# Latent attention with queries in twelve tiles: rotary rows of four heads in one tile, turned with DMA copies and tables, then copied to their heads

## The chip, the cores and the metric

The kernel runs on one core of one Trainium2 chip. The metric is the time of one launch in microseconds of device time. The core has TensorE (PE: matmuls, and their weight loads, PEld), VectorE (DVE), ScalarE (ACT), GpSimd (POOL) and SyncE (SP, which issues most of the DMAs). Each engine works through its own list of instructions in order and waits on semaphores where the list says so.

## The reference

The program has two blocks. The change lies in the first, in the second layer of it, where the mixer is latent attention with 16 heads. For a sequence of 512 positions with 1024 features:

```python
def mla_queries(h, w_q_a, q_a_norm, w_q_b, q_nope_norm, q_rope_norm, cos, sin):
    c_q = rms_norm(h @ w_q_a, q_a_norm)
    q = (c_q @ w_q_b).reshape(bsz, seq, N_HEADS, QK_DIM)
    q_nope = rms_norm(q[..., :QK_NOPE_DIM], q_nope_norm)
    q_rope = apply_rope(rms_norm(q[..., QK_NOPE_DIM:], q_rope_norm), cos[:, :, None, :], sin[:, :, None, :])
    return jnp.concatenate([q_nope, q_rope], axis=-1).transpose(0, 2, 1, 3)

def apply_rope(x, cos, sin):
    x1, x2 = jnp.split(x.astype(jnp.float32), 2, axis=-1)
    return jnp.concatenate([x1 * cos - x2 * sin, x1 * sin + x2 * cos], axis=-1).astype(x.dtype)
```

A head's query has 64 rows without position ("nope") and 32 rotary ones ("rope"). Keys are made likewise, with one rotary part shared by all heads. Then comes causal softmax attention over blocks of 128 queries, and the output product with `w_o`. All of it is in float32.

## The kernel before

Activations lie with features on the 128 partitions and the 512 positions along the row, so one tile is 128x512. A float32 product is made of three matmuls on split values: each weight block is split into a high part `wh` (ScalarE, line 678) and a low part `wl` (VectorE, line 1253), and `product` (lines 2027 to 2029) runs high by high, high by low and low by high for each of its row blocks: three blocks for queries (nine matmuls), two for keys (six). Loads of weight blocks are in a ring of four, the split parts in a ring of two, so block b + 2 can be split only when block b has been used. `ahead(st, i, u, last)` is the split of block u + 2. The blocks of this stage ("b") stand in `BLOCKS_B`.

A query tile of one head has its 64 nope rows, its 32 rope rows, and 32 rows more in which the rope rows stand exchanged (the weights hold them twice). So there is one tile for each head, 16 in all, and the rotation needs no movement: the tile is multiplied by a table (`qtab`), and the doubled rows are summed by the score matmul itself, since the keys hold the shared rope rows twice. One key tile holds the nope rows of two heads (8 tiles).

The order is written out by hand for each engine. For head h, TensorE does: the product for head h + 2 (`head_queries`), then for each of four blocks j of queries `turn_probs(h, j)` (transposes, line 2268) and `scores(h + 1, j)` (lines 2254, 2255); behind j = 1 the mean square of the new query tile by a matmul (`query_mean`, line 2325), in even heads the weighing of values (line 2282), in odd heads the key product of a later pair and its mean (line 2331). ScalarE makes squares (lines 940, 945), inverse roots (lines 702, 703), exponentials (line 874) and copies of transposed probabilities (line 966). VectorE makes the row minima (`row_least`, line 1574; scores are kept negated), the shares (`share_first`, `share_probs`, line 1584: probabilities divided by their sum), queries (`head_queries`, lines 1669, 1671) and keys (`head_keys`, line 1676). `turn_probs(h, 0)` on TensorE needs the first share of head h, and the shares of head h stand behind `row_least(h, 3)` in VectorE's list; this is the loop through which each head hangs on the one before. In VectorE's list for head h stand, in order:

```python
                    share_first(h)
                    ahead(st, 0, AT_B["q", h + 2], True)
                    row_least(h + 1, 0)
                    row_least(h + 1, 1)
                take_sums(h, slice(3, 4))
                share_probs(h, 3)
                    output_low(pair - 1)
                    head_queries(h + 2)
                    row_least(h + 1, 2)
                copy_turned(h)
                    row_least(h + 1, 3)
```

(some conditions left out). Bank 2 of the matmul memory takes query tiles, bank 3 key tiles, bank 7 all means. In the last two heads TensorE also begins the output product (`output_part(u, ks)`, lines 2366 to 2368; a step is one of eight row blocks of one of eight tiles, three matmuls). GpSimd does nothing in this stage.

## Time and profile before

| | |
|---|---|
| median of 3 runs (lowest, highest) | 1868.06 us (1867.62, 1868.92) |
| the profiled execution: its time | 1866.67 us |
| the profiled execution: its span | 1864.6 us |
| mean granted TensorE clock | 0.99 |
| TensorE busy | 1810.5 us (97%) |
| VectorE, ScalarE, GpSimd busy | 1041.5, 839.4, 199.6 us |

The span reaches from the first to the last instruction that the profiler saw; the time has what lies around it too. The rows of the trace below are of the profiled execution. A row of the timeline gives the start from the beginning of the span and the duration, both in microseconds, then the engine, the line, the operation, output and inputs, the shape and how many instructions are merged in it; in square brackets is the idle time before it and what ended it.

### The profile page before, as it was taken

How to read it: one execution, taken by the hardware profiler on the slowest of the kernel's cores; microseconds unless marked ns; L12 is line 12 of the kernel's file. 1: busy time of each engine (PE TensorE's matmuls, PEld its weight loads, DVE VectorE, ACT ScalarE, POOL GpSimd, SP SyncE). 2: the span in 40 equal slices, each digit the busy share in tenths (PEclk: the TensorE clock that was granted, in tenths of full speed). 3: DMA queues.
4: the chain of work that ended last, by engine and by line, in shares of the span. 5: the costliest groups of instructions: out<-in, count | busy, mean ns of one | idle time of the engine just before them, and what ended most of it. 6: DMA issues, size and time to landing. Idle time of an engine off the chain costs nothing.

```text
span 1864.6 us, 24367 instructions
## 1 busy us (share of the span) xinstructions
PE 1810.5 (97%) x8934; PEld 1395.1 (75%) x8934; DVE 1041.5 (56%) x1633; ACT 839.4 (45%) x1406; POOL 199.6 (11%) x269
## 2 busy tenths in 40 slices
PE   9889999999999999999999999999999989999997
PEld 6677778888887766677888888768666767866675
DVE  8874454444334767755444434465555476556647
ACT  5423344443224666644444422232567633265753
POOL 7970000000000000000000000023000012200000
PEclk9989999999999999999999999999999999999998
DMA  6322322323333111122232333323111122311111
GB/s 212 103 58 79 98 94 90 101 91 98 94 96 101 44 35 28 62 74 96 90 101 92 98 94 94 97 87 106 57 57 46 46 90 88 105 51 52 57 45 57
DMA packets 58764, 152.21 MB, mean 82 GB/s; under 512 B 17152, under 2 KB 22048, under 8 KB 58672
## 3 DMA queue, kind: packets, MB, share of 16 engines
q1 hardware_dynamic: 55120, 148.27, 25.3%
q0 software_dynamic: 3552, 2.70, 0.5%
q8 instruction: 59, 0.97, 0.2%
q14 instruction: 33, 0.27, 0.0%
HBM read 143.79 MB, written 4.19 MB: 79 GB/s over the span
## 4 chain that ended last, share of the span: by engine, by line
PE 88%; DVE 4%; ACT 3%; POOL 3%; issue 1%; DMA 0%; SPq 0%; DVEq 0%; ACTq 0%; POOLq 0%
PE bank L2027 19%; PE bank L2028 18%; PE bank L2029 18%; PE bank L2522 3%; PE bank L2524 3%; PE bank L2523 3%; PE bank L2499 2%; PE bank L2487 2%; PE bank L2486 2%; PE bank L2485 2%; PE bank L2254 1%; PE bank L2282 1%; PE bank L2609 1%; PE bank L2537 1%; PE bank L2506 1%
## 5 line engine op out<-in xcount | busy, mean ns | idle before, releaser
L1253 DVE TENSOR_TENSOR wl<-raw,wh 128x1024 fp32r<-128x1024 f32 (+3 forms) x280 | 324.1, 1158 | 493.9 <-ACT wh L678 490.7
L678 ACT ACTIVATE wh<-raw 128x1024 fp32r<-128x1024 f32 (+3 forms) x280 | 279.2, 997 | 573.5 <-PE bank L2029 498.0
L2027 PE MATMUL bank<-xH,wh 128*128 128x512 f32 x904 | 355.2, 393 | 3.9 <-DVE wl L1253 2.1
L2029 PE MATMUL bank<-xH,wl 128*128 128x512 f32 x904 | 352.1, 389 | 0.0
L2028 PE MATMUL bank<-xL,wh 128*128 128x512 f32 x904 | 352.1, 389 | 0.0
L2027 PEld LDWEIGHTS bank<-xH,wh 128*128 128x128 f32 x904 | 169.9, 188 | 43.4 <-DVE xL L1259 3.2
L2028 PEld LDWEIGHTS bank<-xL,wh 128*128 128x128 f32 x904 | 170.0, 188 | 35.6 <-issue 1.0
L2029 PEld LDWEIGHTS bank<-xH,wl 128*128 128x128 f32 x904 | 169.8, 188 | 35.5
L2027 PE MATMUL bank<-hidH,wh 128*128 128x512 f32 x352 | 137.3, 390 | 0.0
L2029 PE MATMUL bank<-hidH,wl 128*128 128x512 f32 x352 | 136.9, 389 | 0.0
L2028 PE MATMUL bank<-hidL,wh 128*128 128x512 f32 x352 | 136.9, 389 | 0.0
L2522 PE MATMUL bank<-xH,wh 128*128 128x512 f32 x256 | 108.4, 423 | 0.0
L2524 PE MATMUL bank<-xH,wl 128*128 128x512 f32 x256 | 100.8, 394 | 0.0
L2523 PE MATMUL bank<-xL,wh 128*128 128x512 f32 x256 | 100.2, 391 | 0.0
L614 POOL TENSOR_TENSOR xT<-xT,acc 128x512 f32<-128x512 f32 x9 | 11.2, 1273 | 737.1 <-ACT acc L1053 737.1
L1925 DVE TENSOR_REDUCE least<-bank 128x1 f32<-128x128 f32 (+3 forms) x96 | 42.6, 485 | 73.4 <-PE bank L2506 73.3
L1109 ACT ACTIVATE Pm<-bank,least 128x128 f32<-128x128 f32 (+3 forms) x96 | 49.8, 524 | 68.3 <-DVE least L1925 68.3
L2028 PEld LDWEIGHTS bank<-hidL,wh 128*128 128x128 f32 x352 | 66.1, 188 | 14.0 <-issue 0.2
L2027 PEld LDWEIGHTS bank<-hidH,wh 128*128 128x128 f32 x352 | 66.1, 188 | 13.9 <-issue 0.2
L2029 PEld LDWEIGHTS bank<-hidH,wl 128*128 128x128 f32 x352 | 66.1, 188 | 13.7
L861 ACT ACTIVATE hidH<-T 128x512 f32 (+1 forms) x44 | 27.8, 632 | 78.3 <-DVEq L1541 78.3
L604 POOL COPY xT<-T 128x512 f32<-128x512 f32 x8 | 8.8, 1105 | 453.3 <-DVE T L1559 453.3
(450 smaller groups left out, 3305.6 us busy)
## 6 DMA issues: line engine op xcount, KB each, us to landing
raw<-w_gu_dram SPq DMA_DIRECT2D x88, 512.0 KB, 3.3
raw<-w_p_dram SPq DMA_DIRECT2D x64, 512.0 KB, 3.4
raw<-w_dn_dram SPq DMA_DIRECT2D x32, 448.0 KB, 3.3
raw<-w_glu_dram SPq DMA_DIRECT2D x16, 512.0 KB, 3.5
raw<-w_dn_dram SPq DMA_DIRECT2D x16, 512.0 KB, 3.5
raw<-w_out_dram SPq DMA_DIRECT2D x16, 512.0 KB, 3.3
raw<-w_in_dram SPq DMA_DIRECT2D x8, 512.0 KB, 7.8
raw<-w_o_dram SPq DMA_DIRECT2D x8, 512.0 KB, 3.4
```

Of the source, the lines that this page charges most:

```text
L678: nc.scalar.activation(wh[:, (st.base + u) % 2, 0:kts * P], raw[:, (st.base + u) % 4, 0:kts * P], ACT.Copy).then_inc(w_high, 1)
L1109: nc.scalar.activation(Pm[side][:, POFF[j]:POFF[j] + w], banks[side][:, 0:w], ACT.Exp, scale=-1.0, bias=least[:, j, side:side + 1], accum_ ...
L1253: nc.vector.tensor_tensor(wl[:, s, 0:kts * P], raw[:, (st.base + u) % 4, 0:kts * P], wh[:, s, 0:kts * P].bitcast(F32), ALU.subtract).then_ ...
L1925: nc.vector.tensor_reduce(least[:, j, side:side + 1], banks[side][:, 0:(j + 1) * P], AX, ALU.min)\
L2027: nc.tensor.matmul(bank, wh[:, s, w], hi[:, k, :], start=first and kt == 0, stop=False)
L2028: nc.tensor.matmul(bank, wh[:, s, w], lo[:, k, :], start=False, stop=False)
L2029: ins = nc.tensor.matmul(bank, wl[:, s, w], hi[:, k, :], start=False, stop=last and kt == kts - 1)
L2485: nc.tensor.matmul(o, xH[:, k, rows], wh[:, s, w], start=k == 0, stop=False)
L2486: nc.tensor.matmul(o, xH[:, k, rows], wl[:, s, w], start=False, stop=False)
L2522: nc.tensor.matmul(bank, wh[:, s, w], xH[:, kt, :], start=kt == 0, stop=False)
L2523: nc.tensor.matmul(bank, wh[:, s, w], xL[:, kt, :], start=False, stop=False)
L2524: ins = nc.tensor.matmul(bank, wl[:, s, w], xH[:, kt, :], start=False, stop=kt == KD - 1)
```

## The change

Queries are packed without doubled rows. Eight tiles ("n") hold the nope rows of two heads each, four tiles ("r") the rope rows of four heads each: first halves of the four heads in the upper 64 rows, second halves in the lower 64. That makes 12 query tiles. The nope halves go from the bank straight to the heads' query tiles (`take_queries`, two operations over 64 rows). A rope tile is taken with its norm to `rope_q` (`take_rope`), GpSimd issues two DMA copies that write its halves exchanged to `rope_x`, VectorE multiplies both by tables and adds them (`turn_rope`), and GpSimd issues eight DMA copies of 16 rows that place the result in four heads' query tiles, four for each pair. The tables are built from the sine table by sixteen DMA copies. The query tiles are now four instead of two, with the unused rows zeroed once. TensorE's order gives a head one projection from `MAIN` (rope tile 1 for head 0, then nope queries in odd heads and keys in even ones), and heads 3 and 7 a second one from `SECOND` (rope tiles 2 and 3); output steps begin in head 13. The means take one matmul for each tile as before. Scores wait for `rope_placed` too.

```diff
-BLOCKS_B = [("q", 0), ("k", 0), ("v", 0), ("v", 1), ("q", 1), ("k", 1)]
-for _p in range(1, NH // 2):
-    BLOCKS_B += [("q", 2 * _p), ("q", 2 * _p + 1)] + [("k", _p + 1)] * (_p + 1 < NH // 2)
+BLOCKS_B = [("r", 0), ("k", 0), ("v", 0), ("n", 0), ("v", 1), ("k", 1), ("n", 1), ("r", 1), ("n", 2), ("k", 2), ("n", 3),
+            ("r", 2), ("k", 3), ("n", 4), ("k", 4), ("n", 5), ("r", 3), ("k", 5), ("n", 6), ("k", 6), ("n", 7), ("k", 7)]
+IN_BANK2 = [("r", 0)] + [("n", p) for p in range(NH // 2)]
+IN_BANK3 = [b for b in BLOCKS_B if b[0] != "v" and b not in IN_BANK2]
+NORMED = [b for b in BLOCKS_B if b[0] != "v"]
+MAIN = dict(enumerate([("r", 1)] + [(kind, p) for p in range(2, NH // 2) for kind in "nk"]))
+SECOND = {3: ("r", 2), 7: ("r", 3)}
 AT_B = {kind: n for n, kind in enumerate(BLOCKS_B)}
...
-    qst = [mla.tensor(f"qst{b}", [P, S]) for b in range(2)]
+    qst = [[mla.tensor(f"qst{s}", [P, S])[:, :] for s in range(2)], [sq[:, s, :] for s in range(2)]]
     qtab = [mla.tensor(f"qtab{s}", [P, S]) for s in range(2)]
+    rope_q, rope_x = T[:, 1, :], sd[:, :]
...
             pool.dma_start(posI[:, :], pos.to_broadcast([P, S])).then_inc(sem("pos_loaded"), 16)
             pool.dma_start(means[:, :], con[:, CON["mean_even"][0]:CON["fold"][1]]).then_inc(sem("means_loaded"), 16)
+            pool.wait_ge(sem("rope_table"), 1)
+            for n in range(8):
+                to = slice(n * DR // 2, (n + 1) * DR // 2)
+                turning = DN + DR + n // 4 * DR // 2
+                pool.dma_start(qtab[0][to, :], ropeT[DN:DN + DR // 2, :]).then_inc(sem("rope_rows1"), 16)
+                pool.dma_start(qtab[1][to, :], ropeT[turning:turning + DR // 2, :]).then_inc(sem("rope_rows1"), 16)
+            for g in range(NH // 4):
+                pool.wait_ge(sem("roped"), 2 * g + 1)
+                for half in range(2):
+                    pool.dma_start(rope_x[half * DN:(half + 1) * DN, :], rope_q[(1 - half) * DN:(2 - half) * DN, :])\
+                        .then_inc(sem("rope_rows0"), 16)
+                pool.wait_ge(sem("roped"), 2 * g + 2)
+                for pair in range(2 * g, 2 * g + 2):
+                    if pair >= 2:
+                        pool.wait_ge(sem("scores_ready"), 8 * pair - 8)
+                    for s in range(2):
+                        for half in range(2):
+                            to = (DN, 0)[s] + half * DR // 2
+                            at = half * DN + (2 * (pair % 2) + s) * DR // 2
+                            pool.dma_start(qst[pair % 2][s][to:to + DR // 2, :], rope_q[at:at + DR // 2, :])\
+                                .then_inc(sem(f"rope_placed{pair % 2}"), 16)
...
+            for n, name in enumerate(("q_nope", "q_rope")):
+                step(nc.vector.tensor_scalar(tiny[:, 24 + n:25 + n], column(name), -scale, None, ALU.mult))
+            for tile in qst:
+                step(nc.vector.memset(tile[0][DN + DR:P, :], 0.0))
+                step(nc.vector.memset(tile[1][DR:DN, :], 0.0))
+
+            def take_rope(g):
+                bank, i = taken_from(("r", g))
+                if g:
+                    for n in range(2):
+                        dve.wait_ge(sem(f"rope_placed{n}"), 64 * g)
+                dve.wait_ge(sem("rq_ready" if bank == 2 else "rk_ready"), i + 1)
+                nc.vector.scalar_tensor_tensor(rope_q, banks[bank][:, :], tiny[:, 25:26], (R if bank == 2 else acc)[:, :], ALU.mult, ALU.mult)\
+                    .then_inc(sem("roped"), 1)
+                dve.wait_ge(sem("roped"), 2 * g + 1)
+                dve.sem_inc(sem("q_used" if bank == 2 else "kv_used"), 1)
+
+            def turn_rope(g):
+                if g == 0:
+                    dve.wait_ge(sem("rope_rows1"), 256)
+                dve.wait_ge(sem("rope_rows0"), 32 * (g + 1))
+                step(nc.vector.tensor_tensor(rope_q, rope_q, qtab[0][:, :], ALU.mult))
+                step(nc.vector.tensor_tensor(rope_x, rope_x, qtab[1][:, :], ALU.mult))
+                nc.vector.tensor_tensor(rope_q, rope_q, rope_x, ALU.add).then_inc(sem("roped"), 1)
+
+            take_rope(0)
+            dve.wait_ge(sem("krope_folded"), 1)
             dve.wait_ge(sem("krope_folded"), 1)
             def rope_rows(p):
                 step(nc.vector.tensor_copy(kst[p][0][bottom, :], banks[6][bottom, :]))
                 step(nc.vector.tensor_copy(kst[p][1][top, :], banks[6][top, :]))
             rope_rows(0)
-            def head_queries(h):
-                s = h % 2
-                dve.wait_ge(sem("rq_ready"), h + 1)
-                step(nc.vector.tensor_tensor(qst[s][:, :], banks[2][:, :], R[:, :], ALU.mult))
+            def take_queries(pair):
+                dve.wait_ge(sem("rq_ready"), taken_from(("n", pair))[1] + 1)
+                for s, rows in enumerate((top, bottom)):
+                    step(nc.vector.scalar_tensor_tensor(qst[pair % 2][s][rows, :], banks[2][rows, :], tiny[rows, 24:25], R[rows, :],
+                                                        ALU.mult, ALU.mult))
                 dve.sem_inc(sem("q_used"), 1)
-                nc.vector.tensor_tensor(qst[s][:, :], qst[s][:, :], qtab[s][:, :], ALU.mult).then_inc(sem("qk_ready"), 1)
-
...
-                if h + 2 < NH:
-                    head_queries(h + 2)
-                if s and pair + 2 < NH // 2:
-                    ahead(st, 0, AT_B["k", pair + 2], True)
+                if h in MAIN:
+                    take(MAIN[h])
+                if h in SECOND:
+                    ahead(st, 0, AT_B[SECOND[h]], True)
+                if h in (1, 4, 8):
+                    turn_rope(1 + h // 4)
                 if h + 1 < NH:
                     row_least(h + 1, 2)
                 copy_turned(h)
                 if h + 1 < NH:
                     row_least(h + 1, 3)
+                if h in SECOND:
+                    take(SECOND[h])
...
+                sooner = NORMED[0:NORMED.index(item)]
+                pe.wait_ge(sem("qsq_ready" if bank == 2 else "ksq_ready"), i + 1)
+                if sooner:
+                    pe.wait_ge(sem("rq_ready"), sum(b in IN_BANK2 for b in sooner))
+                    if any(b in IN_BANK3 for b in sooner):
+                        pe.wait_ge(sem("rk_ready"), sum(b in IN_BANK3 for b in sooner))
                 else:
                     pe.wait_ge(sem("latroot_ready"), 3)
-                nc.tensor.matmul(banks[7][:, :], mean_of("mean_odd" if h % 2 else "mean_even"), T[:, 0, :], start=True, stop=True)\
-                  .then_inc(sem("qstat_ready"), 1)
-
-            def key_mean(pair):
-                pe.wait_ge(sem("ksq_ready"), pair + 1)
-                pe.wait_ge(sem("rq_ready"), max(2 * pair, 1))
-                nc.tensor.matmul(banks[7][:, :], mean_of("mean_pair"), T[:, 2, :], start=True, stop=True)\
-                  .then_inc(sem("kstat_ready"), 1)
+                mean = mean_of("mean_rope" if item[0] == "r" else "mean_pair")
+                nc.tensor.matmul(banks[7][:, :], mean, T[:, 0 if bank == 2 else 2, :], start=True, stop=True)\
+                  .then_inc(sem("qstat_ready" if bank == 2 else "kstat_ready"), 1)
             def values(m):
...
                 for j in range(QT):
                     turn_probs(h, j)
                     if h + 1 < NH:
                         scores(h + 1, j)
-                    if j == 1 and h + 2 < NH:
-                        query_mean(h + 2)
+                    if j == 1 and h in MAIN:
+                        mean_square(MAIN[h])
                     if pair and s == 0 and j in (1, 2):
                         weigh(pair - 1, range(2 * j - 2, 2 * j))
-                    if s and pair + 2 < NH // 2:
+                    if h in SECOND:
                         if j == 1:
-                            pair_keys(pair + 2)
+                            projected(SECOND[h])
                         if j == 2:
-                            key_mean(pair + 2)
+                            mean_square(SECOND[h])
                     if h == NH - 2 and j == 3:
                         output_part(0, range(4, 6))
                     if h == NH - 1 and j % 2:
-                        output_part(1, range(j - 1, j + 1))
+                        output_part(1, range(j + 1, j + 3) if j == 1 else range(4, 5))
             weigh(NH // 2 - 1, range(QT))
-            output_part(0, range(6, KD))
-            output_part(1, range(4, KD))
+            output_part(0, range(6, 7))
+            output_part(1, range(5, 7))
```

TensorE in odd head 5, from the mean behind j = 1: before, the six matmuls of a key product (`cvH`, `cvL`) and at the end its mean stand among turns and scores.

```order
L2325 MATMUL bank<-T,means 128x512 [waits rk_ready,rq_ready,qsq_ready]
L2027 MATMUL bank<-cvH,wh 128x512 [waits w_split,kv_used]
L2028 MATMUL bank<-cvL,wh 128x512
L2029 MATMUL bank<-cvH,wl 128x512
L2027 MATMUL bank<-cvH,wh 128x512
L2028 MATMUL bank<-cvL,wh 128x512
L2029 MATMUL bank<-cvH,wl 128x512
L2268 MATMUL bank<-cons,Pb_103 128x128 [waits turned_act,probs_shared]
L2268 MATMUL bank<-cons,Pb_103 128x128 x2
L2254 MATMUL bank<-kst_120,qst_122 128x384 [waits probs_ready]
L2255 MATMUL bank<-causal,minus_unit 128x128
L2331 MATMUL bank<-T,means 128x512 [waits rq_ready,ksq_ready]
```

After, nothing stands there, and the key product comes once the head is done:

```order
L2393 MATMUL bank<-T,means 128x512 [waits rk_ready,rq_ready,qsq_ready]
L2334 MATMUL bank<-cons,Pb_103 128x128 [waits turned_act,probs_shared]
L2334 MATMUL bank<-cons,Pb_103 128x128 x2
L2320 MATMUL bank<-kst_120,sq 128x384 [waits probs_ready]
L2321 MATMUL bank<-causal,minus_unit 128x128
L2334 MATMUL bank<-cons,Pb_103 128x128 [waits turned_act,probs_shared]
L2334 MATMUL bank<-cons,Pb_103 128x128 x3
L2320 MATMUL bank<-kst_120,sq 128x512 [waits probs_ready]
L2321 MATMUL bank<-causal,minus_unit 128x128
L2092 MATMUL bank<-cvH,wh 128x512 [waits w_split,kv_used]
```

The product and the mean have moved to the even heads, and the query product that opened the even head now opens the odd one.

VectorE in head 3, from the queries to the first shares of head 4 (`Pb`), before:

```order
L1669 TENSOR_TENSOR qst_123<-bank,R 128x512 [waits rq_ready]
L1671 TENSOR_TENSOR qst_123<-qst_123,qtab_125 128x512 [waits dve_steps]
L1253 TENSOR_TENSOR wl<-raw,wh 128x384 [waits w_high]
L1574 TENSOR_REDUCE nmax<-bank 128x1 [waits scores_ready]
L1592 COPY PTc<-bank 128x4x128 [waits transposed]
L1574 TENSOR_REDUCE nmax<-bank 128x1 [waits scores_ready]
L1579 RECIPROCAL rden<-den 128x3 [waits probs_ready]
L1584 TENSOR_SCALAR Pb_102<-Pb_102,rden 128x128 [waits dve_steps]
```

and after, where lines 1602, 1607, 1612 and 1620 are the minimum, the reciprocal, the share and the copy:

```order
L1720 SCALAR_TENSOR_TENSOR sq<-bank,tiny,R 64x512 [waits rq_ready]
L1720 SCALAR_TENSOR_TENSOR sq<-bank,tiny,R 64x512 [waits dve_steps]
L1282 TENSOR_TENSOR wl<-raw,wh 128x384 [waits dve_steps,w_high]
L1602 TENSOR_REDUCE nmax<-bank 128x1 [waits scores_ready]
L1620 COPY PTc<-bank 128x4x128 [waits transposed]
L1602 TENSOR_REDUCE nmax<-bank 128x1 [waits scores_ready]
L1696 SCALAR_TENSOR_TENSOR T<-bank,tiny,acc 128x512 [waits rk_ready,rope_placed1,rope_placed0]
L1607 RECIPROCAL rden<-den 128x3 [waits roped,probs_ready]
L1612 TENSOR_SCALAR Pb_102<-Pb_102,rden 128x128 [waits dve_steps]
```

The third line from the end is new: `take_rope(2)`, which waits for its own root (`rk_ready`), stands between the last minimum and the shares.

GpSimd behind the loads of this stage, before (the next is work of the second block):

```order
L607 DMA posI_117<-pos_dram 128x512 [waits hid_used0]
L608 DMA means_127<-con_dram 128x512
L614 TENSOR_TENSOR xT_49<-xT_49,acc_59 128x512 [waits ln_sq,ln_delta_copied]
L614 TENSOR_TENSOR xT_49<-xT_49,acc_59 128x512 x2
L619 DMA rope_cos_144<-con_dram 128x512
```

and after, from the last two of the sixteen table copies on:

```order
L621 DMA qtab0_124<-ropeT_116 16x512
L622 DMA qtab1_125<-ropeT_116 16x512
L626 DMA sd_60<-T_62 64x512 [waits roped]
L626 DMA sd_60<-T_62 64x512
L636 DMA qst0_122<-T_62 16x512 [waits roped]
L636 DMA qst0_122<-T_62 16x512
L636 DMA qst1_123<-T_62 16x512 x2
L636 DMA sq_61<-T_62 16x512 x4
```

The exchange waits for `roped` once, the placing copies once more; pair 0's four and pair 1's four follow one another.

## Rows read from the trace of the kernel before

**Rows 1.** The page, part 1: busy time, share of the span, instructions.

```profile
PE 1810.5 (97%) x8934; PEld 1395.1 (75%) x8934; DVE 1041.5 (56%) x1633; ACT 839.4 (45%) x1406; POOL 199.6 (11%) x269
```

**Rows 2.** Windows: one pair of heads, busy time (instructions), clock, DMA share, GB/s.

```profile
713.87:732.69 18.82, 18.46 (x92) 12.02 (x91) 13.89 (x34) 13.30 (x35) 0.00 (x0) 1.00 0.11 29
```

**Rows 3.** Timeline, TensorE: start, us, line, form, count; heads 3 and 4.

```profile
686.92 0.45 PE L2027 MATMUL bank<-cqH,wh 128*128 128x512 f32 x1
...
689.08 0.27 PE L2268 MATMUL bank<-cons,Pb 128*128 128x128 f32 x1
...
690.21 1.07 PE L2325 MATMUL bank<-T,means 128*128 128x512 f32 x2
...
694.09 1.13 PE L2331 MATMUL bank<-T,means 128*128 128x512 f32 x2 [0.36 <-ACT T L945]
...
698.55 0.27 PE L2268 MATMUL bank<-cons,Pb 128*128 128x128 f32 x1
```

**Rows 4.** Timeline, VectorE: one large split, then heads 2 and 3.

```profile
635.48 1.23 DVE L1253 TENSOR_TENSOR wl<-raw,wh 128x1024 fp32r<-128x1024 f32 x1
...
682.33 1.53 DVE L1676 SCALAR_TENSOR_TENSOR kst<-bank,vecs,acc 64x512 f32<-64x512 f32 x2
684.01 0.69 DVE L1669 TENSOR_TENSOR qst<-bank,R 128x512 f32<-128x512 f32 x1
684.85 0.69 DVE L1671 TENSOR_TENSOR qst<-qst,qtab 128x512 f32<-128x512 f32 x1
...
690.80 0.61 DVE L1574 TENSOR_REDUCE nmax<-bank 128x1 f32<-128x128 f32 x2
...
693.58 0.69 DVE L1669 TENSOR_TENSOR qst<-bank,R 128x512 f32<-128x512 f32 x1 [0.98 <-ACT R L703]
...
695.50 0.55 DVE L1574 TENSOR_REDUCE nmax<-bank 128x1 f32<-128x384 f32 x1
...
697.41 0.88 DVE L1584 TENSOR_SCALAR Pb<-Pb,rden 128x128 f32<-128x128 f32 x3
```

**Rows 5.** Timeline, TensorE: a mean, first scores, turn of head 1.

```profile
631.45 1.02 PE L2294 MATMUL bank<-sq,means 128*128 128x512 f32 x2
632.33 0.47 PE L2027 MATMUL bank<-cvH,wh 128*128 128x512 f32 x1
...
646.10 0.38 PE L2254 MATMUL bank<-kst,qst 128*128 128x128 f32 x2
...
670.22 0.33 PE L2268 MATMUL bank<-cons,Pb 128*128 128x128 f32 x1 [0.48 <-DVE Pb L1584]
```

**Rows 6.** Timeline, ScalarE: the sine of the rotary table, a large split.

```profile
619.21 0.63 ACT L917 ACTIVATE ropeT<-ropeT 128x512 f32<-128x512 f32 x1
...
634.39 1.05 ACT L678 ACTIVATE wh<-raw 128x1024 fp32r<-128x1024 f32 x1
```

**Rows 7.** Timeline, GpSimd: one of sixteen issues in a row.

```profile
1289.00 0.50 POOL L639 DMA_DIRECT2D cq_exact<-fg_low  x1
```

**Rows 8.** DMA issues: copies between rows, KB each, median us to landing.

```profile
acc<-qk POOLq DMA_DIRECT2D x32, 16.0 KB, 3.2
```

**Rows 9.** Timeline, TensorE: turn of head 13, last output steps, the product behind.

```profile
783.18 0.27 PE L2268 MATMUL bank<-cons,Pb 128*128 128x128 f32 x1
...
807.55 0.50 PE L2366 MATMUL bank<-kvH,wh 128*128 128x512 f32 x1 [0.53 <-DVE kvL L1702]
...
811.26 0.38 PE L2428 MATMUL bank<-tiny,cons 64*128 64x4 f32 x2
```

**Rows 10.** Timeline, TensorE: two gaps earlier in the kernel.

```profile
69.70 1.89 PE L2079 MATMUL bank<-G,C 128*32 128x128 f32 x32 [2.74 <-DVEq L1419]
...
149.55 0.47 PE L2027 MATMUL bank<-zH,wh 128*128 128x512 f32 x1 [1.16 <-DVE wl L1253]
```

**Rows 11.** Windows behind these gaps; the number after POOL is the clock.

```profile
69.00:74.00 5.00, 4.30 (x39) 3.27 (x40) 4.62 (x6) 0.39 (x1) 4.84 (x3) 0.66 0.15 56
148.00:153.00 5.00, 3.84 (x17) 2.85 (x16) 3.81 (x4) 3.09 (x4) 0.00 (x0) 1.00 0.44 129
```

254 lines of the change are left out of this document (132 added, 122 removed).

## The prediction

> **What bounds the kernel now.** I read the page first: TensorE is busy 1810.5 of 1864.6 us, VectorE 56%, ScalarE 45% [rows 1]. So what counts is the TensorE work that goes and the waits that come, in the attention stage, 632 to 811 us. Next the windows by pair of heads: in steady state a pair takes 18.82 us, TensorE 18.46 of them, VectorE 13.89, ScalarE 13.30 [rows 2]. TensorE binds, but the other two are at 74% and 71%, and they work in series on one chain per head, so I followed that chain in the timelines.
>
> TensorE in odd head 3 [rows 3]: a query product starts at 686.92, the turning of the head's probabilities (line 2268, "turn") at 689.08, the mean square at 690.21, then come the pair's key product (six matmuls for nine: 1.44 us) and, after a wait of 0.36, its mean at 694.09, the next query product, and the next turn at 698.55. Turn to turn is 9.47 us; the even half of a pair is 18.82 less that, 9.35.
>
> The chain in the same head, in VectorE's timeline [rows 4]: ScalarE squares the finished product and splits the next weights; then VectorE reads row minima at 690.80 (1.7 behind the turn); ScalarE takes two exponentials and the root; VectorE forms the queries at 693.58 (2.78 behind the minima). Behind them in its queue stand a weight split, the minimum of the third score row (695.50), a copy, the last minimum and the shares (697.41); a third of these 0.88 us lets the next turn go, at about 697.72. So the chain is 8.65 us from turn to turn, 0.8 shorter than TensorE's work. That 0.8 is all the cover there is.
>
> **What is removed.** Four query tiles. A tile costs TensorE 686.92 to 689.08, 2.16 us, and its mean 631.45 to 632.33, 0.88 [rows 3, 5]. 4 x 3.04 = 12.2 us. If TensorE stayed full, the profiled execution's 1866.67 would become 1854.5. VectorE counts level: 16 x 2 operations of 128x512 make room for 8 x 2 half-height and 4 x 4 full ones, and four splits go. Half height buys nothing: the pair's two key operations over 64 rows take 682.33 to 684.01, 1.68 us, as two full ones do [rows 4].
>
> **What moves, and why the gain does not come through.** The new order gives a head one projection: nope queries in odd heads, keys in even ones, and rotary tiles beside them in heads 3 and 7. An even head keeps its weighing of values and is followed by a query product: 9.35 us of TensorE as before, above the chain. An odd head has lost its key product, its key mean and (the next product being keys) a third of a query product: 9.47 - 1.44 - 0.9 - 0.36 - 0.7 = 6.1 us of work (the terms: key product, mean, its wait, 2.16 - 1.44). Its chain is hardly shorter: the 8.65 of before, less the split and the two operations in front of the minimum (695.50 - 693.58 = 1.92), plus 1.68 for the halves: 8.4. So the odd head takes 8.4, with TensorE idle about 2.4 just before each turn.
> - Plain pairs (heads 5 and 6, 9 and 10): 8.4 + 9.35 = 17.8, 1.0 less than before: -2.0. Heads 11 and 12: the odd one has no split and takes 7.6, the even one waits 0.5 for its squares behind the large split, and 4 steps of the output product are moved here (+0.7): 18.2, -0.7.
> - Pairs with a rotary tile (3 and 4, 7 and 8): in the odd head the rotary product (2.16) delays the third score row, a split (0.47) goes in front of its minimum, and before the shares VectorE must wait for a second root and then take the tile (0.8): the root cannot start before the third exponential, 7.8 us behind the turn, ends at 9.1, the take at 10.0, the turn at 10.5. In the even head, taking keys (1.68) is followed by the turning, three 128x512 operations at 0.84, 0.84 and 0.61 (684.01 to 684.85 is the first of such [rows 4]): 2.3 more before the minima, so that the chain there, about 9.9, passes TensorE's 9.35. 20.4 for the pair: +1.6 each, +3.2.
> - Heads 1 and 2: the turning is in the odd head: 8.4 + 2.3 - 0.1 = 10.6, and 9.35: +1.1.
>
> Heads 1 to 12 together: +1.6.
>
> **The start.** Work moves forward: up to head 1's turn TensorE does seven tiles, not six, and one mean more: +3.0. On top come new waits. Block 4 (the second half of the values) can be split only when block 2 is used up, at 643, not at 634: ready at 645.4 by 1.05 us on ScalarE and 1.23 on VectorE [rows 4, 6]. The first rotary tile is taken by 639.4 (its root ends at 638.0 as the first root does now, four memsets stand before it), its two swap copies are issued in 1.0 and land by 643.5, the turning stands behind that split in VectorE's queue, ends 647.7, and four copies to the heads take 2.0 to issue. One GpSimd copy issue holds 0.50 us, and a copy from rows to rows lands 3.2 us after its issue [rows 7, 8]: 652.5. TensorE has by then just finished the values, so first scores come at 652.5 for 646.10 [rows 5], with almost no wait for the copies. Then the mean of tile (n, 1) must wait until the root of (k, 1) has freed the bank, behind the third exponential of head 0: 2.8 us idle near 660. Head 1's turn I get at 674.5, against 670.22 [rows 5]: +4.3.
>
> The sixteen table copies start when the sine is done (619.85 [rows 6]) and need 8.0 + 3.2: 631, long before 645. The later rotary tiles are copied a head or more before their scores; their wait is hidden by about 9 us of other work, and would cost the exposed 4 x 0.5 + 3.2 = 5.2 each if that went. The Trainium skill (DMA: Bandwidth & Descriptors, Anatomy of one DMA) puts a GpSimd copy at about 2.0 us plus bytes over 436 GB/s, so 2.1 for 32 KB; the trace's 3.2 disagrees upward and is what I use; by the page nothing in the sum would move, because the values end at 652.4 anyway.
>
> **The tail.** From head 13's turn (783.18) to the last output step (811.26, the small product behind it) are 28.1 us [rows 9]. Of these go the last query mean (0.88), the four output steps now done before that turn (2.85), the 0.53 at 807.55 for the low half of the last pair (three steps stand in front of it now, one before), and about 0.7 of small waits, among them that for the query bank: -5.0.
>
> **TensorE's clock.** In this kernel a gap of 2.74 us ended at 69.70, and 69 to 74 then ran at a mean granted clock of 0.66 (down to 1.2 GHz), a loss of 5 x 0.34 = 1.7 us; a gap of 1.16 at 149.55 left it at 1.00, 2.4 GHz [rows 10, 11]. In the attention stage the granted clock is 1.00 now [rows 2]. Head 1 gets one of 10.6 - 6.1 = 4.5, right before an even head that TensorE binds: +1.7. The one at 660 gives about +0.5 more. The odd gaps of 2.4 lie between the two observations, nearer to 2.74; I count them at nothing, and at 1.7 each in the range.
>
> **Sum.** +4.3 + 1.6 - 5.0 + 2.2 = +3.1 us on 1866.67. The median of the runs shown is 1868.06, 1.4 above the profiled execution, and the change goes on it: 1871. About 0.2% (3.7 us) is what a measurement of this kernel tells from no change.
>
> **Rivals.**
> - *TensorE stays full.* For it: 97% busy, every microsecond of work removed counts, and my odd-head chain has only to be 1.5 us shorter. Against: the cover of 0.8 us. All of it gives 1855.9; half of the removed work comes through if the two rotary pairs run like plain ones (-5.2) and the start costs only its work (-1.3, and no clock loss, -2.2): 1862. Chance 0.14.
> - *The clock falls in every odd head.* One mechanism: each odd gap of about 2.4 us lets the clock fall, and the even head behind it, bound by TensorE, starts slow. Heads 3, 5, 7, 9 and 11: up to 5 x 1.7 = 8.5, 1879; with two of them 1874. It decides from where half a drop more (0.8 us) is added. For it: 2.74 was enough. Against: 1.16 was not, and heads 3, 7 and 11 leave only 1.5 to 1.8. With errors of the start and the rotary pairs to the same side: 0.41.
> - *The copies come late.* If the four placing copies took 3 us more at the start, scores wait 3: 1874; later ones never show. It is inside the case above. The Trainium skill (same page, SWDGE vs HWDGE vs iDMA) says VectorE's two-port operations keep GpSimd from writing descriptors; that would stretch the 0.50 us of an issue. The row shows 0.50; no run here shows it beside such operations.
> - *Forecast:* the waits eat the gain, 1867 to 1871.8: 0.45.
>
> Range: 1863 to 1877. It leaves the full gain and four or more clock drops outside.
>
> **What would show it.** Right: pairs of about 17.8 (plain) and 20.4 (rotary) us; TensorE idle released by VectorE's shares at the turns of heads 2, 4, 6, 8, 10; first scores 21 us behind the first product's end; a low clock after head 1's gap; the tail 5 us shorter. Wrong: a pair under 17 us (chain overestimated), a wait on the rope copies at a score row (copies late), or clock below 1.00 after each odd head.

## The result and the profile after

The changed kernel takes 1885.13 us (median of 4 runs, 1881.43 to 1886.83), the kernel before 1867.84 beside it (4 runs): ratio 1.0086, 95% interval 1.0074 to 1.0098. It is slower by 17.3 us; the forecast was 3 slower, 1871, in a range that ended at 1877. One execution among all those reported below, in the third kernel of experiments 9 to 11, took 2565.27 us at a mean granted clock of 0.65 and stays out of every comparison.

The profiled execution of after takes 1886.83 us, its span 1885.0 (before 1866.67 and 1864.6). Page, part 1, as in [rows 1]:

```profile
PE 1812.5 (96%) x8890; PEld 1394.4 (74%) x8890; DVE 1044.3 (55%) x1631; ACT 832.0 (44%) x1389; POOL 228.0 (12%) x325
```

There are 44 matmuls fewer, and TensorE is busy 2 us longer: less work, more time for it. The next rows say where; "..." stands for rows left out, here and in all that follows. They are TensorE's timeline of after: the stage's first mean, the first scores, gaps, and the first turn (one transpose, L2334) of heads 1, 2, 3, 4, 6, 7, 10 and 13; then the small product behind the output and the product after it.

```profile
635.40 0.59 PE L2360 MATMUL bank<-sq,means 128*128 128x512 f32 x1
...
656.90 0.46 PE L2320 MATMUL bank<-kst,qst 128*128 128x128 f32 x2 [0.41 <-PE bank L2409]
...
665.75 0.67 PE L2393 MATMUL bank<-T,means 128*128 128x512 f32 x1 [2.69 <-ACT acc L732]
...
678.89 0.33 PE L2334 MATMUL bank<-cons,Pb 128*128 128x128 f32 x1 [0.67 <-DVE Pb L1612]
...
689.60 0.48 PE L2334 MATMUL bank<-cons,Pb 128*128 128x128 f32 x1 [4.34 <-DVE Pb L1612]
...
701.17 0.27 PE L2334 MATMUL bank<-cons,Pb 128*128 128x128 f32 x1
...
711.30 0.80 PE L2092 MATMUL bank<-cvH,wh 128*128 128x512 f32 x1 [2.54 <-DVEq L1699]
...
714.03 0.41 PE L2334 MATMUL bank<-cons,Pb 128*128 128x128 f32 x1
...
733.55 0.33 PE L2334 MATMUL bank<-cons,Pb 128*128 128x128 f32 x1 [2.29 <-DVE Pb L1612]
...
744.71 0.27 PE L2334 MATMUL bank<-cons,Pb 128*128 128x128 f32 x1
...
776.79 0.33 PE L2334 MATMUL bank<-cons,Pb 128*128 128x128 f32 x1 [2.30 <-DVE Pb L1612]
...
804.76 0.27 PE L2334 MATMUL bank<-cons,Pb 128*128 128x128 f32 x1
...
828.06 0.27 PE L2495 MATMUL bank<-tiny,cons 64*128 64x4 f32 x1
...
829.99 0.47 PE L2092 MATMUL bank<-kvH,wh 128*128 128x512 f32 x1 [1.55 <-DVE wl L1282]
```

Against the same marks of before (631.45, 670.22, 783.18 and 811.26, [rows 5, 9]):

| part | before | after | difference | forecast |
|---|---|---|---|---|
| up to the stage's first mean | 631.45 | 635.40 | +3.95 | 0 |
| from there to head 1's turn | 38.77 | 43.49 | +4.7 | +4.3 |
| head 1's turn to head 13's | 112.96 | 125.87 | +12.9 | +3.3 with the clock |
| head 13's turn to the small product | 28.08 | 23.30 | -4.8 | -5.0 |
| from there to the end (1866.67, 1886.83) | 1055.41 | 1058.77 | +3.4 | 0 |

The forecast's other 0.5 was clock at the start; it belongs to the second row, where the clock did fall (0.64 from 665.75 to 669.75). Start and tail came out as worked out. The middle is four times what was forecast, and two parts that had no term cost 7.3. Call the stretch from first mean to small product the stage: 179.8 us before, 192.7 after.

The clock in after: windows of 4 us (TensorE busy, granted clock, DMA share, GB/s), and one over the stage.

```profile
686.00:690.00 4.00, 0.40 (x2) 0.67 0.11 25
690.00:694.00 4.00, 4.00 (x13) 0.50 0.21 57
694.00:698.00 4.00, 4.00 (x26) 0.98 0.00 0
710.00:714.00 4.00, 2.69 (x6) 0.65 0.29 67
734.00:738.00 4.00, 4.00 (x14) 0.64 0.19 53
777.00:781.00 4.00, 4.00 (x21) 1.00 0.39 111
832.00:836.00 4.00, 4.00 (x14) 0.74 0.33 109
632.00:824.00 192.00, 169.44 (x764) 0.95 0.17 46
```

Behind the gap of 4.34 TensorE was full for 4 us at 0.50, that is 1.2 GHz for 2.4, and did half the work. The clock fell too, for a part of their windows, behind the gaps of 2.54 and 2.29, and behind the 1.55 that ended at 829.99, but not behind the 2.30 that ended at 776.79. Before had 1.00 all through the stage.

### The profile page after: what moved, and what is told of

Its sections match the earlier page's. It is cut to its first block, busy times and chain, and to the rows that moved or that the text cites. A ratio compares the mean times of both kernels' runs of the same rounds, so it can differ in the third digit from the quotient of the medians.

```text
span 1885.0 us, 24327 instructions
## 1 busy us (share of the span) xinstructions
PE 1812.5 (96%) x8890; PEld 1394.4 (74%) x8890; DVE 1044.3 (55%) x1631; ACT 832.0 (44%) x1389; POOL 228.0 (12%) x325
## 4 chain that ended last, share of the span: by engine, by line
PE 84%; DVE 7%; ACT 4%; POOL 3%; issue 2%; DMA 0%; SPq 0%; DVEq 0%; ACTq 0%; POOLq 0%
PE bank L2092 18%; PE bank L2093 18%; PE bank L2094 18%; PE bank L2589 3%; PE bank L2591 3%; PE bank L2590 3%; PE bank L2566 2%; PE bank L2552 2%; PE bank L2554 2%; PE bank L2553 2%; DVE wl L1282 1%; PE bank L2676 1%; PE bank L2604 1%; PE bank L2320 1%; PE bank L2573 1%
```

## Experiments

Eleven kernels and a second trace of the kernel before. Stage times are read as above, in each run's own trace. A head is measured from its own first turn to the next head's.

### 1. Two waits taken away by order

VectorE and ScalarE handle the second tile of heads 3 and 7 sooner, and the output product ends its first block sooner:

```diff
+                    if j == 2 and h in SECOND:
+                        root_of(SECOND[h])
                     if h + 1 < NH:
                         probs(h + 1, 1 - s, j)
...
-                    if j == 2 and h in SECOND:
-                        root_of(SECOND[h])
...
                     row_least(h + 1, 2)
+                if h in SECOND:
+                    take(SECOND[h])
                 copy_turned(h)
                 if h + 1 < NH:
                     row_least(h + 1, 3)
-                if h in SECOND:
-                    take(SECOND[h])
...
-            output_part(1, range(5, 7))
+            output_part(1, range(5, 6))
             output_part(0, range(7, KD))
-            output_part(1, range(7, KD))
+            output_part(1, range(6, KD))
```

> Two waits of the changed kernel that the prediction did not have are taken away by order alone. (1) In heads 3 and 7 ScalarE forms the rotary tile's root before the third exponential (it sat idle 1.50 us there) and VectorE takes the tile before the copy and the fourth minimum, so bank 3 comes free about 2 us sooner for the key product of heads 4 and 8, whose gap is 2.54 us now. (2) At the end block 0 of the output product is finished three steps before block 1, so the split of block 2 is ready sooner (gap 1.55 us now). Theory 'the two waits and the clock fall behind each are most of the excess': the gaps at heads 4 and 8 fall to 0.5 us, the granted clock stays at 1.00 in 710 to 718 and 754 to 762, each pair with a rotary tile is 2 to 3 us shorter, the tail 1 to 2; in all 5 to 8 us less behind the start of the stage. Rival 'the chain of VectorE sets the head anyway, the product only fills its idle time': the gap moves from in front of the key product to in front of the next turn, 0 to 2 us less. On the part before the stage both say nothing; if its extra 4 us against the kernel before are chance they need not come back here.

Measured: 1879.74 us in one run, stage 190.2 (2.5 less), heads 1 to 13 123.3 (2.6 less), from the small product to the end 1055.45, the 1055.41 of before. The key product's gap, and the one behind the output (no clock fall follows it now):

```profile
708.83 0.50 PE L2092 MATMUL bank<-cvH,wh 128*128 128x512 f32 x1 [1.03 <-DVEq L1699]
...
825.53 0.47 PE L2092 MATMUL bank<-kvH,wh 128*128 128x512 f32 x1 [0.85 <-DVE wl L1282]
```

Heads 3 and 4 take 20.8 us for 23.2, heads 7 and 8 20.9 for 22.9; against that stands a fall of the clock in head 10 (11.19 for 9.55), which moved here. Behind the output the next product starts 1.24 us after the small one, for 1.93 in after and 0.31 in before: 1.6 of the 3.4 there were the wait, and 0.9 of it is left; another 1.5 was the fall of the clock. The small rest, 0.3, arises later, where the executions differ by themselves (see 9 to 11), and that is also why this trace ends level with before. Both waits are real. The total fell by 5.8 us, within the 5 to 8 of the first theory, though the two gaps fell to 1.03 and not to 0.5; the rival allowed at most 2.

### 2. The gaps filled with products that nobody needs

```diff
+            def filler(count, pair):
+                if count and pair > 1:
+                    pe.wait_ge(h_ready, 32 + pair - 1)
+                for _ in range(count):
+                    nc.tensor.matmul(banks[6][:, :], const("ones"), cons[:, 0:S], start=True, stop=True)
```

> The changed kernel with extra products into a bank that is free (ones times constants, 0.59 us each, nothing reads them) in the seven gaps of TensorE from the start of the stage to head 12: 4 ahead of the second nope tile's mean, 7 ahead of head 2's turn, 4 ahead of the key products of heads 4 and 8, 3, 3 and 2 ahead of the turns of heads 6, 10 and 12. Nothing else changes, so the chains stay as long as they are. Theory 'the clock': with no gap the granted clock stays at 1.00 all through the stage, and what the gaps cost behind them comes back: 1.7 us or more for each of the six falls of this part (666 to 762 us), stage 6 to 9 us shorter. Rival 'the waits alone': the clock may stay up but the chains on VectorE and ScalarE set the end, stage shorter by less than 2 us or even longer by the fillers that end late.

Measured: 1880.60 us in one run, stage 189.8, 2.9 less. One window over the stage, of this kernel:

```profile
640.00:820.00 180.00, 174.14 (x790) 1.00 0.15 43
```

The clock theory's first half holds: TensorE is busy 174 of 180 us here (169 of 192 in after's window above), and was done sooner with more to do. The heads behind a gap show it: head 2 takes 9.35 us for 11.57, head 6 9.39 for 11.16. The size was missed (2.9 for 6 to 9), because a filler is two instructions and took 0.86 us, not 0.59 (seven took 6.01). So the seven ahead of head 2's turn made head 1 take 12.2 for 10.7, and the four ahead of head 4's key product made head 3 12.3 (head 7 too; with the wait but no fall it takes 11.64, as in experiment 4). Experiment 5 repeats it with numbers that fit.

### 3. No rotation

The three VectorE operations of `turn_rope` (line 1699 on) are left out, so queries go unrotated to their heads.

> Leaves out the rotation of the queries: the three VectorE operations over 128x512 per group of four heads (12 in all); the copies stay. Theory 'the rotation stands in the chain of its head': heads 1, 4 and 8 are each about 2.2 us shorter (0.72+0.72+0.72), and the first score rows come up to 2.2 us sooner. Rival 'hidden': the even heads 4 and 8 are bound by TensorE or by the wait for bank 3, so they get under 1 us shorter; only head 1 gains. Everything from head 9 on as it was.

Measured: 1877.46 us in one run, stage 189.4; head 1 8.76 us for 10.71, head 4 9.63 for 10.37, head 8 9.87 for 10.68. The first scores came 21.5 us behind the first mean, as in after: they wait for the last of the values in both (0.41, the row at 656.90 of after). So the rival was right of the even heads, and the rotation costs nothing at the start.

Neither theory had the next thing: heads 5 and 9, which have no rotation, take 8.62 and 8.61 us for 9.15. ScalarE's last exponential of head 9 and its part of the weight split, and VectorE's first minimum (head 9's turn stands at 758.36):

```profile
757.12 0.69 ACT L903 ACTIVATE Pb<-bank,nmax 128x512 f32<-128x512 f32 x1 [1.29 <-DVE nmax L1602]
...
759.05 0.52 ACT L707 ACTIVATE wh<-raw 128x384 fp32r<-128x384 f32 x1
```

```profile
760.07 0.61 DVE L1602 TENSOR_REDUCE nmax<-bank 128x1 f32<-128x128 f32 x2
```

and the same two of ScalarE in after (turn at 767.64):

```profile
767.22 0.69 ACT L903 ACTIVATE Pb<-bank,nmax 128x512 f32<-128x512 f32 x1 [0.52 <-DVE nmax L1602]
...
768.85 0.53 ACT L707 ACTIVATE wh<-raw 128x384 fp32r<-128x384 f32 x1
```

Without the rotation TensorE's own work sets the end of head 8, as it did in before: the exponential starts 1.24 us ahead of the turn, the split 0.69 behind it, the minimum 1.71 behind it, the 1.7 of [rows 3, 4]. With it the shares set that end (0.20 idle at the turn of head 9, 0.57 at that of head 5), the exponential starts only 0.42 ahead, the split 1.21 behind, the minimum 2.25 behind. So the rotation costs 4.6 us in five heads (1.95, 0.74, 0.53, 0.81, 0.54); the stage is only 3.3 shorter, since the clock fell in heads 10 and 12 instead of head 6.

### 4. Twice the copies

```diff
+                            pool.dma_start(ropeT[at:at + DR // 2, :], rope_q[at:at + DR // 2, :])\
+                                .then_inc(sem(f"rope_placed{pair % 2}"), 16)
                             pool.dma_start(qst[pair % 2][s][to:to + DR // 2, :], rope_q[at:at + DR // 2, :])\
```

(the waits on `rope_placed` doubled).

> The changed kernel with each placing copy of GpSimd preceded by a second one of the same size and source into a tile that is free, so a pair of heads needs eight issues, not four. At the start the last copy lands about 2.0 us later (4 x 0.49). Theory 'no slack at the start, plenty later': first scores 1.5 to 2.5 us later, all heads from 1 on as long as they were, stage +2. Rival 'copies are on the path in the rotary heads too': heads 4, 5, 8 and 9 get longer by 1 us or more each. If they were hidden at the start as well: stage within 0.5 us.

Measured: 1886.27 us in one run, stage 192.0, 0.7 less than after, with one fall of the clock fewer. The first scores wait for the copies now, 21.9 us behind the first mean for 21.5:

```profile
656.99 0.35 PE L2324 MATMUL bank<-kst,qst 128*128 128x128 f32 x1 [0.79 <-DMA qst<-T]
```

Both theories missed in part: 2 us more of copies cost 0.4 at the start, not 1.5 to 2.5, and heads 4, 5, 8 and 9 did not get longer. The rows of after say why there was slack: a copy of 32 KB landed 1.8 us after its issue there (median of sixteen), not 3.2.

```profile
sd<-T POOLq DMA_DIRECT2D x8, 128.0 KB, 2.2
qst<-T POOLq DMA_DIRECT2D x16, 32.0 KB, 1.8
```

The rival of late copies is out. The Trainium skill (DMA: Bandwidth & Descriptors, Anatomy of one DMA) gave an estimate of 2.1 us for such a copy. The 1.8 of these rows is closer to it than to the 3.2 of [rows 8] that the prediction used. Those were copies of half the size, 16 KB, so size is not what made them slower; what did is not shown.

### 5. Waits taken away and gaps filled to measure

The first experiment's orders, with fillers that fit: 3 at the start, 5 ahead of head 2's turn, 1 ahead of the key products of heads 4 and 8, 2 ahead of the turns of heads 6, 10 and 12.

> The two waits taken away as in the first experiment, and extra products (0.82 us each as measured) that fit into the gaps: 3 at the start, 5 ahead of head 2's turn, 1 ahead of the key products of heads 4 and 8, 2 ahead of the turns of heads 6, 10 and 12. The seven and four of the filler experiment ended 1.4 and 0.7 us behind what TensorE waited for. Theory 'waits and clock are separate sums': the granted clock stays at 1.00 in the whole stage; from the stage's first mean to the small product behind the output (192.7 us in the changed kernel, 190.2 without the two waits) it takes 184 to 186, and the total is 1874 to 1876. Rival 'the clock is only seen where TensorE has slack': 188 to 190, total 1878 to 1880. Neither brings it to the kernel before (179.8).

Measured: 1875.94 us (4 runs), ratio to before 1.0043 (1.0026 to 1.0060); stage 184.5, clock 1.00, heads 1 to 13 117.6. All as the first theory said. Against experiment 1, which differs by the fillers alone, heads 1 to 13 are 5.65 us shorter: that is what the clock cost there.

### 6. Orders alone

On top of the first experiment's orders:

```diff
+            root_of(("k", 1))
             probs(0, 0, 2)
-            root_of(("k", 1))
             root_of(("n", 1))
...
+                if h + 1 < NH:
+                    row_least(h + 1, 0)
+                    row_least(h + 1, 1)
                 if h < NH - 5:
                     ahead(st, 0, AT_B[MAIN[h]], True)
                 elif NH - 4 <= h < NH - 2:
                     ahead(st, 0, AT_B[MAIN[h - 1]], True)
-                if h + 1 < NH:
-                    row_least(h + 1, 0)
-                    row_least(h + 1, 1)
```

> No extra products; orders only. The two waits taken away; the root of key tile 1 ahead of head 0's third exponential, so bank 7 is free for the next mean (gap 2.69 us at the start); and in every head VectorE reads the first two row minima ahead of its weight split, where it stood waiting for ScalarE's half of the split (1.24 us in head 9). Theory 'the odd head is the chain behind its turn, 9.15 us, of which 0.7 are the split's place': odd heads 5 and 9 take 8.5 to 8.7 us, the start 2 us less; stage 184 to 187 us with clock falls still in it, total 1874 to 1877. Rival 'the split is needed as soon': TensorE waits at the next product for the split instead, odd heads stay at 9.1 and a gap by a weight split (wl) shows. Worse: shorter work with the same gaps makes the clock fall more often.

Measured: 1871.54 us (10 runs), ratio 1.0022 (1.0012 to 1.0031), stage 183.4, odd heads 5 and 9 8.37 us, the start 2.5 less. Better than expected. VectorE's timeline of head 9, first in after (turn at 767.64), then with these orders (turn at 751.05; the trace is that of experiment 7):

```profile
769.41 0.56 DVE L1282 TENSOR_TENSOR wl<-raw,wh 128x384 fp32r<-128x384 f32 x1 [1.23 <-ACT wh L707]
769.89 0.62 DVE L1602 TENSOR_REDUCE nmax<-bank 128x1 f32<-128x128 f32 x2
...
772.67 1.54 DVE L1720 SCALAR_TENSOR_TENSOR qst<-bank,tiny,R 64x512 f32<-64x512 f32 x2 [0.97 <-ACT R L732]
774.45 0.56 DVE L1602 TENSOR_REDUCE nmax<-bank 128x1 f32<-128x384 f32 x1 [0.24 <-DVE qst L1720]
...
776.44 0.88 DVE L1612 TENSOR_SCALAR Pb<-Pb,rden 128x128 f32<-128x128 f32 x3
```

```profile
751.82 0.29 DVE L1602 TENSOR_REDUCE nmax<-bank 128x1 f32<-128x128 f32 x1 [0.24 <-PE bank L2321]
752.55 0.42 DVE L1602 TENSOR_REDUCE nmax<-bank 128x1 f32<-128x256 f32 x1 [0.44 <-PE bank L2321]
752.89 0.55 DVE L1282 TENSOR_TENSOR wl<-raw,wh 128x384 fp32r<-128x384 f32 x1
...
755.30 1.53 DVE L1720 SCALAR_TENSOR_TENSOR qst<-bank,tiny,R 64x512 f32<-64x512 f32 x2 [0.67 <-ACT R L732]
```

In after the first minimum stands 2.25 us behind the turn, held up by the split in front of it; with the new order 0.77, and the queries 4.25 behind the turn for 5.03. That is the 0.78 that the head gets shorter.

### 7. Orders and fillers

> The orders of the run before it and the fitted extra products (none at the start). Theory: both gains add: stage 181 to 184 us, total 1869 to 1873: the change at its best here, and still no faster than the kernel before by 0.2%, since odd heads stay bound by their chain and the start is 3 us longer. Rival: under 179.8 us, faster than before.

Measured: 1868.33 us (10 runs), ratio 1.0005 (0.9995 to 1.0014), stage 179.6. Better than the theory (181 to 184, total 1869 to 1873). The stage is at the rival's limit of 179.8, but the total is level with the kernel before and not faster; heads 1 to 13 take 114.7 us, 2.9 less than in experiment 5.

### 8. The kernel before again

> The kernel before once more, for a second trace. The stage's first mean came at 631.45 in its first trace, and in the changed kernel and its variants, whose instructions up to there are the same but for one wait of GpSimd, at 635.40, 634.13, 632.31, 631.80 and 635.11. Theory 'chance of the first transfers and of what VectorE and GpSimd make of each other': this trace may lie anywhere in 631 to 635. Rival 'something in the changed program makes the part before the stage later': 631.4 to 631.6 again.

Measured: 1870.96 us, the stage's first mean at 636.47, every head of the stage as in the first trace, stage 179.8. So the extra time is not the changed program's, and the spread is wider than the first theory's 631 to 635; its causes (transfers, VectorE and GpSimd) are not shown. Windows of before's first trace, of after, and of this one, all over the same code (TensorE busy, granted clock, DMA share, GB/s):

```profile
60.00:80.00 20.00, 17.08 (x178) 0.91 0.24 72
...
120.00:140.00 20.00, 19.30 (x277) 1.00 0.24 77
```

```profile
60.00:80.00 20.00, 15.53 (x162) 1.00 0.21 68
...
120.00:140.00 20.00, 19.30 (x249) 0.83 0.24 77
```

```profile
60.00:80.00 20.00, 15.54 (x163) 1.00 0.24 78
...
120.00:140.00 20.00, 18.62 (x234) 0.83 0.25 77
```

The part before the stage runs in several patterns, and the granted clock between 120 and 140 us tells them apart. Over all fourteen traces the first mean lies between 631.45 and 636.47: at 631.45 to 632.31 in the seven with a clock of 1.00 there, at 633.13 to 634.48 in the three with 0.91 to 0.93, at 635.09 to 636.47 in the four with 0.83. Before itself shows the first and the last. The profiled execution of after had the last; its 3.95 us belong to no step of the change.

### 9 to 11. The rotation on GpSimd

```diff
+                if g:
...
+                    pool.wait_ge(sem("rope_rows0"), 32 * (g + 1))
+                    step(nc.gpsimd.tensor_tensor(rope_q, rope_q, qtab[0][:, :], ALU.mult))
+                    step(nc.gpsimd.tensor_tensor(rope_x, rope_x, qtab[1][:, :], ALU.mult))
+                    nc.gpsimd.tensor_tensor(rope_q, rope_q, rope_x, ALU.add).then_inc(sem("roped"), 1)
...
-                if h in (1, 4, 8):
-                    turn_rope(1 + h // 4)
```

On after alone, then on experiment 7 (with 3 fillers ahead of head 2's turn for 5), then on experiment 6:

> The changed kernel with that one edit alone: the three later rotations on GpSimd. Theory: head 1 about 2 us shorter, heads 4 and 8 0.7 each, and the clock falls may shift; stage 188.5 to 190 for 192.7. Rival (engines in each other's way): stage 192 or more, VectorE's operations beside GpSimd's longer than the 0.68 of a 128x512 copy.

> The orders and fitted extra products of the version that drew level with the kernel before (stage 179.6 us), and the rotation of the three later groups of heads on GpSimd instead of VectorE (three operations over 128x512 each; the first group stays on VectorE, since the first scores wait for it). Without any rotation heads 1, 4 and 8 were 1.95, 0.74 and 0.8 us shorter. Theory 'the rotation stands in VectorE's chain and GpSimd has time for it': head 1 takes 8.4 to 8.6 for 10.35 and heads 4 and 8 9.4 to 9.5 for 9.87, stage 176.5 to 177.5, total 1865 to 1866. Rival 'the two engines get in each other's way': GpSimd's operations take 2 us and more, VectorE's beside them longer too; stage 179 or more.

> Orders and GpSimd rotation, without the extra products: all work in it is needed. Theory 'clock': it keeps one or two falls of about 2 us each, stage 179 to 181, total 1867 to 1869, level with the kernel before. Rival 'with head 1's gap cut from 3.75 to about 2 us no fall is left there': stage 177 to 178, and the total under 1866.

Measured: the first 1877.38 us in one run, stage 186.9, head 1 9.28 us for 10.71 (1.4 less, not 2); the stage is 1.6 us better than the best expected, with one fall of the clock fewer and heads 5 and 9 at 8.61 as in experiment 3. The second 1866.31 us (11 runs), ratio 0.9998 (0.9989 to 1.0007), stage 176.8, head 1 9.39, heads 4 and 8 9.51. The third 1866.85, ratio 0.9994 (0.9985 to 1.0003), stage 177.4, as its rival had it, with one fall (in head 6) and none behind head 1, but the total is not under 1866.

The stage of the second is 3.0 us shorter than that of before, as expected, but the total is not: in its trace the part behind the stage took 1058.0 us for 1055.4, which undoes most of it. 0.9 of that is the wait left behind the output (experiment 1). The rest comes in the same code, 0.7 between 1165 and 1230 us and 0.6 between 1540 and 1595. Behind 1165 us the executions differ by themselves: the second trace of before is 0.8 faster there than the first, the third kernel of this section loses 1.6, and the first, with the same rotation, 0.4. What moves them is open. So the best versions are level with the kernel before within the interval, and none is shown to be faster.

Head 1 takes 8.14 us in the third kernel for 9.97 in experiment 6, 1.8 less, near the 1.95 of experiment 3. (In the second, three fillers ended late: 9.39.) Collisions of the rival's kind are there. This one is in the second kernel, GpSimd's rotation in head 1 and VectorE's share of the fourth row:

```profile
674.69 1.47 POOL L633 TENSOR_TENSOR sd<-sd,qtab 128x512 f32<-128x512 f32 x1
```

```profile
675.14 1.30 DVE L1619 TENSOR_SCALAR Pb<-Pb,rden 128x512 f32<-128x512 f32 x1
```

That operation takes 0.49 us elsewhere in the stage. Here it began inside GpSimd's and ended 0.3 us behind it, and so it did in all three rotations of the second and of the third kernel (1.30 to 1.32 us) and in two of the first's (0.77 and 0.78, begun later): wherever it began, it ended 0.3 us behind GpSimd's operation. The Trainium skill (SBUF — State Buffer, SBUF: two separate sides) says that GpSimd and a VectorE operation in a two-port mode take their shared pair of ports in turn, each for a whole instruction. The ends in these rows agree with that; which mode this VectorE operation ran in no row shows. It lost 0.8 us each time and did not decide: the chain got shorter by more.

### 12. Key products behind the first turn

On the second of those kernels, without the fillers of heads 4 and 8:

```diff
-                if h in MAIN:
+                if h in MAIN and h - 1 not in SECOND:
                     projected(MAIN[h])
...
+                    if j == 0 and h - 1 in SECOND:
+                        projected(MAIN[h])
```

(ScalarE's squares and split behind the first exponential.)

> On top of the orders, the rotation on GpSimd and the fitted extra products (stage 176.8 us): in heads 4 and 8 TensorE makes the key product behind the first turn and first score row of the head instead of ahead of them, so that it no longer stands waiting for bank 3 (1.03 us each); ScalarE squares it behind the first exponential. Theory 'the last bank waits are real idle time that work can fill': each pair with a rotary tile 0.7 to 1.0 us shorter, stage 174.8 to 175.5, total 1863 to 1865, just about faster than the kernel before. Rival 'the key product's own chain (squares, root, keys) sets the even head': what head 3 gains head 4 loses, stage 176.5 to 177.5.

Measured: 1871.37 us (11 runs), ratio 1.0016 (1.0007 to 1.0025), stage 181.4, 4.6 worse than the second kernel above. TensorE at head 4's turn:

```profile
704.66 0.33 PE L2342 MATMUL bank<-cons,Pb 128*128 128x128 f32 x1 [2.81 <-DVE Pb L1622]
```

Head 3 takes 10.42 us as without this edit, head 4 11.14 for 9.51 at a clock of 1.00, head 8 12.55, with a fall of the clock. The 1.03 us in front of the key product had not been what set head 3; it lay inside the longer wait for the shares. The product had stood in idle time, and now stands in head 4's own time. The first theory is out. The rival had the direction, but not the size, and head 3 did not gain what it had it gain.

## Why the prediction was wrong

**The odd head's chain.** "So the odd head takes 8.4, with TensorE idle about 2.4 just before each turn" is the step that failed first. Its place was right (idle time ended by VectorE's shares, 2.29 and 2.30), its size 0.75 too small: heads 5 and 9 took 9.15. The chain of before was measured from a turn that TensorE made 0.8 late, so ScalarE was by then 1.23 us past the start of the last exponential. In heads 5 and 9 of after the turn follows the shares at once, because the rotation in the even head ahead of them ("so that the chain there, about 9.9, passes TensorE's 9.35") had used up that lead: the exponential starts 0.42 ahead of the turn, and the output's upper half, the squares and the split stand behind it. First minimum 2.25 behind the turn for the 1.7 of [rows 3, 4], the rest nearly as worked out (queries 2.78 behind the minimum, 1.78 for the halves, 2.0 for the end). Experiment 3 shows it: with the rotation out the minimum is back at 1.71, and the head takes 8.61, near the 8.4. The prediction had both numbers and did not carry the one into the other. Experiment 6 got 0.78 back another way, by taking away the split in front of the minimum. Without clock and bank waits heads 1 to 13 cost +4.65 (experiment 5, two gaps of 1.03 still in it) for +1.6.

**The pairs with a rotary tile.** "The take at 10.0, the turn at 10.5" was right of the take (the key product that it releases starts 10.1 behind the turn) and missed who waits: the tile stands in bank 3, and the next key product goes into the same bank. That product came 2.54 and 2.53 us late, and the turn behind it. Both facts were there in the order of instructions, and I did not follow the bank. Cost without its clock: 1.2 each (head 3 takes 11.64 in experiment 4, where no fall came behind the wait, and 10.42 in experiment 5), 2.4 in all.

**The clock.** "The odd gaps of 2.4 lie between the two observations; I count them at nothing" was the costly choice: 12.9 less 4.65 and 2.4 leaves 5.8 us in heads 1 to 13 for 1.7 (experiments 1 and 5, which differ by fillers alone, measure 5.65). A fall costs about what the prediction took, 1.7: head 6 takes 11.16 with one, 9.5 without; head 2 lost 2.0, the pairs with a rotary tile 1.2 and 0.9. What was wrong is how often. Counted over the stage's gaps from head 2's turn on, in the traces without fillers (after, experiments 1, 3, 4, 6 and the first and third of 9 to 11): of 3.75 to 4.34 us, all 4 were followed by a fall; of 2.52 to 2.54, 6 in 8; of 2.28 to 2.39, 8 in 12; of 2.02, 1 in 2; of 1.70 to 1.80, 2 in 9. The rival "the clock falls in every odd head", with a chance of 0.41, came nearest: of its five heads three had a fall in after (5, and 3 and 7, whose gap was the bank's and not the chain's), 9 and 11 had none. It ended at 1879, and would have been too small even with all five, because the chain, the bank and the output's order were not in it.

**Behind the output.** No term. "Three steps stand in front of it now" saw only the step's own wait. The first block of the output product now ends one step before the second, where it ended four steps before it, and the third can be split only when the first is used up: 1.55 us idle and a fall behind it, 3.1 of the 3.4. Experiment 1 ends the first block one step sooner: 0.9 is left and no fall. In experiment 3 the same 1.55 brought no fall, and that trace lost 1.6 here: half of this term was chance.

**What held.** The start (+4.7 for +4.3 and 0.5 of clock; the gap ahead of the second nope tile's mean 2.69 for 2.8; first scores 21.5 us behind the first mean, 21.05 forecast), head 1 (10.71 for 10.6), heads 11 and 12 (18.4 for 18.2), the tail (-4.8 for -5.0), and that no score row waits for copies later on.

The sum: 4.7 + 4.65 + 2.4 + 5.8 - 4.8 + 3.4 = 16.2 of stage and what follows, and 3.95 by chance in front, 20.2 in the profiled execution. The medians differ by 17.3: the profiled execution of before lies 1.2 below its median, that of after 1.7 above.

## What to carry to other kernels

When work is taken from the engine that binds, measure the next chain from what releases it, not from when the full engine got to it: the other engines' queues had a lead that goes too, here because of work added one head earlier. Then follow every buffer of a moved product to its next writer. And an idle gap on TensorE costs more than its length, even where the chain would have waited anyway: twelve gaps of 2.28 to 2.39 us brought eight falls of 1.4 to 1.7, so removing a tile (3.0 us) and leaving gaps can cost more than the tile. With orders to match and the rotation on GpSimd the same change costs nothing that these runs can tell (the third of experiments 9 to 11, no filler in it), but no faster version was shown.

## What was not expected of the hardware

- The same program runs the part before the stage in patterns up to 5 us apart (first mean at 631.45 and 636.47), told apart by TensorE's granted clock between 120 and 140 us (1.00 and 0.83).
- Whether a gap lets the clock fall is not settled by its length alone: 2.29 us did and 2.30 us did not in one trace.
- A VectorE operation of 0.49 us took up to 1.32 beside one of GpSimd and ended 0.3 us behind it in all eight cases of experiments 9 to 11, while GpSimd's issues of copies kept their 0.5 us (0.48 to 0.54).
